# HGRN2 elementwise work on VectorE instead of GpSimd, and a new order of the input projection's columns

## The reference

```python
h = rms_norm(x, norm_pre_mix[l])
proj = jnp.einsum('btd,de->bte', h, w_in[l])        # 3400 columns, the last 2048 are hq, hf, hi, hg
...
f = lb + (1.0 - lb) * jax.nn.sigmoid(hf)
logf = jnp.log(f)
k = 1.0 - f
q = jax.nn.silu(hq)
# S_t = diag(f_t) S_{t-1} + k_t v_t^T,  o_t = S_t^T q_t   (v = hi)
o = rms_norm(o, out_gain) * jax.nn.silu(hg)
```

## Time and profile before

| | us |
|---|---|
| median of 3 runs | 3892.73 (3880.02 to 3896.85) |
| profiled execution, its time | 3889.4 |
| profiled execution, its span | 3887.5 |
| PE busy in the span | 3430.1 (88%) |
| DVE busy | 1858.7 (48%) |
| ACT busy | 1480.8 (38%) |
| POOL busy | 795.1 (20%) |

### The profile page before, as it was taken

One profiled execution on the slowest core, in us unless ns is written; L12 is line 12 of the kernel. 1 busy time (PEld: TensorE's weight loads), 2 busy tenths in 40 slices (PEclk: granted clock), 3 DMA queues, 4 the chain that ended last, 5 costly groups with the idle time before them and its releaser, 6 DMA issues. The chain is left out here.

```text
span 3887.5 us, 45027 instructions
## 1 busy us (share of the span) xinstructions
PE 3430.1 (88%) x17952; PEld 2966.0 (76%) x17952; DVE 1858.7 (48%) x2624; ACT 1480.8 (38%) x2010; POOL 795.1 (20%) x825
## 2 busy tenths in 40 slices
PE   8898998896657788788888897999999999999998
PEld 8898888895646667666667786888788878887887
DVE  3343444443447878888886333332333233323332
ACT  3433434333335555566665433222222222223221
POOL 0456575666731121010000010000000000000000
PEclk9999999998866878989998998999999999999999
DMA  5333232222110000000000344223323332323232
GB/s 181 130 121 110 94 139 96 105 104 74 35 43 20 21 20 11 18 13 11 11 4 4 140 169 155 90 96 135 114 102 116 121 116 98 125 103 119 98 119 87
DMA packets 82982, 336.70 MB, mean 87 GB/s; under 512 B 7264, under 2 KB 28384, under 8 KB 64352
## 3 DMA queue, kind: packets, MB, share of 16 engines
q1 hardware_dynamic: 75872, 312.96, 22.8%
q10 hardware_dynamic: 6912, 20.97, 1.4%
HBM read 272.50 MB, written 61.41 MB: 86 GB/s over the span
## 5 line engine op out<-in xcount | busy, mean ns | idle before, releaser
L1852 PE MATMUL ps_dense<-h_hi,wd_hi 128*128 128x512 f32 x1408 | 551.9, 392 | 31.5 <-DVE h_lo L1802 19.1
L1853 PE MATMUL ps_dense<-h_lo,wd_hi 128*128 128x512 f32 x1408 | 550.9, 391 | 0.0
L1854 PE MATMUL ps_dense<-h_hi,wd_lo 128*128 128x512 f32 x1408 | 550.8, 391 | 0.0
L1796 DVE TENSOR_TENSOR wd_lo<-wd_raw,wd_hi 128x2048 fp32r<-128x2048 f32 (+1 forms) x136 | 303.3, 2230 | 499.8 <-ACT wd_hi L1751 499.8
L667 PE MATMUL PJ<-w_hi,h_hi 128*128 128x342 f32 (+1 forms) x1280 | 423.7, 331 | 4.2 <-DVE w_lo L548 4.2
L668 PE MATMUL PJ<-w_lo,h_hi 128*128 128x342 f32 (+1 forms) x1280 | 415.7, 325 | 0.0
L669 PE MATMUL PJ<-w_hi,h_lo 128*128 128x342 f32 (+1 forms) x1280 | 414.6, 324 | 0.0
L1751 ACT ACTIVATE wd_hi<-wd_raw 128x2048 fp32r<-128x2048 f32 (+1 forms) x136 | 252.5, 1857 | 405.6 <-PE ps_dense L1874 234.7
L1317 PE MATMUL SC<-V,pT 128*128 128x64 f32 x2176 | 332.9, 309 | 42.2 <-ACT pT L1055 42.1
L1317 PEld LDWEIGHTS SC<-V,pT 128*128 128x128 f32 x2176 | 310.7, 222 | 77.7 <-ACT pT L1055 77.7
L1852 PEld LDWEIGHTS ps_dense<-h_hi,wd_hi 128*128 128x128 f32 x1408 | 266.0, 189 | 89.6 <-DVE h_lo L1802 19.5
(11 more groups left out here) (209 smaller groups left out, 6702.5 us busy)
## 6 DMA issues: line engine op xcount, KB each, us to landing
wd_raw<-in_w_gu SPq DMA_DIRECT2D x88, 1024.0 KB, 4.8
wd_raw<-in_w_down SPq DMA_DIRECT2D x40, 1024.0 KB, 4.8
w_raw<-in_w_in SPq DMA_DIRECT2D x20, 1368.0 KB, 6.2
w_raw<-in_w_in SPq DMA_DIRECT2D x20, 1352.0 KB, 6.1
row_h<-proj_d SPq DMA_DIRECT2D x16, 1024.0 KB, 7.9
proj_d<-stage SPq DMA_DIRECT2D x40, 342.0 KB, 3.7
proj_d<-stage SPq DMA_DIRECT2D x40, 338.0 KB, 2.6
row<-proj_d SPq DMA_DIRECT2D x16, 676.0 KB, 4.1
```

The lines of the kernel that those rows point to most:

```text
L1796: nc.vector.tensor_tensor(w_lo[:, k % 2, w], w_raw[:, w], w_hi[:, k % 2, w].bitcast(F32), ALU.subtract).then_inc(w_lo_ready, 1)
L1852: nc.tensor.matmul(o, w_hi[:, f % 2, w], h_hi[:, c, :], start=(c == 0), stop=False)
L1853: nc.tensor.matmul(o, w_hi[:, f % 2, w], h_lo[:, c, :], start=False, stop=False)
L1854: last = nc.tensor.matmul(o, w_lo[:, f % 2, w], h_hi[:, c, :], start=False, stop=(c == KD - 1))
```

## The change

1. All of the recurrence's 512-column and larger elementwise work moves from POOL to DVE: `gates`, `log_low`, `tail_keys`, `output_gate`, `ke`, `level_sum`. POOL keeps the `root` and `norm` steps on a few columns. Two pairs of multiply and add become one SCALAR_TENSOR_TENSOR each (`hq` and `gg`), and the three halvings of `level_sum` become one TENSOR_REDUCE over the eight masks, read with a stride of 128 elements, into a new tile `asum`.
2. On PE `output` is split: `carried` (state part) stands right behind `levels`, and `output` (the part that waits for the sum) stands later. A new semaphore `hs_done` tells DVE that `qe` is free.
3. The projection goes by passes: superblocks 0 and 1 as before, then the HGRN2 columns of superblock 2, those of superblock 3, the attention columns of superblock 3, and last those of superblock 2. `begin` becomes 29, 39, 50, 61, 72, 82, 92, 102, 112, and 6 products for each of blocks 8 to 15. There are five loads of x tiles in place of four (20 tiles, not 16), as superblock 2 is normalised and turned twice.

```diff
-    begin = [29 + 10 * b for b in range(13)] + [149 + 11 * n // 4 for n in range(1, 4)] + [NPROD]
+    PASSES = [(0, HG_COLS), (0, AT_COLS), (1, HG_COLS), (1, AT_COLS), (2, HG_COLS), (3, HG_COLS),
+              (3, AT_COLS), (2, AT_COLS)]
+    chunks = [(s, col) for s, cols in PASSES for col in cols]
...
+    begin = [29 + 43 * b // 4 for b in range(4)] + [72 + 10 * b for b in range(4)] + [112 + 6 * b for b in range(9)]
...
-    row_before = [max(PER * (b // 4) + 24, begin[b - 1] + begin[b - 1] % 2 if b >= 2 else 0) for b in range(NB)]
+    row_before = [max(4 * rows_at[b // 4], begin[b - 1] + begin[b - 1] % 2 if b >= 2 else 0) for b in range(NB)]
...
+            def gates(b):
...
+                link(v.tensor_tensor(fg[:], sig[:, 1, :], lb[:, 1, :], ALU.mult))
+                link(v.tensor_tensor(hk[:], lb[:, 1, :], fg[:], ALU.subtract))
+                v.tensor_tensor(fg[:], lb[:, 0, :], fg[:], ALU.add).then_inc(hk_ready, 1)
+                v.scalar_tensor_tensor(hq[:], sig[:, 0, :], 1.0, r[:, H_ROW["q"]:H_ROW["q"] + 512], ALU.add,
+                                       ALU.mult).then_inc(hq_ready, 1)
...
+                link(v.scalar_tensor_tensor(gg[:], sig[:, 2, :], 1.0, z, ALU.add, ALU.mult))
+                v.tensor_tensor(gg[:], gg[:], g_hg[:], ALU.mult).then_inc(gg_ready, 1)
...
-            def level_queries(b, h):
+            def level_operands(b, h):
                 n = HG * b + h
                 wait_pair_read(dve, use[f"decay{h}", b])
                 v.tensor_copy(elast[:, h:h + 1], decay[:, h % 2, NM - 1, P - 1:P])
                 if n >= 2:
-                    dve.wait_ge(ho_done, n - 1)
+                    dve.wait_ge(hs_done, n - 1)
                 v.tensor_tensor(qe[:, h % 2], decay[:, h % 2], hqT[:, h:h + 1, :].broadcast_to([P, NM, P]),
                                 ALU.mult).then_inc(qe_ready, 1)
+                v.tensor_tensor(ke[:, h % 2], decay[:, h % 2, 0:NM - 1, :],
+                                hkT[:, h:h + 1, :].broadcast_to([P, NM - 1, P]), ALU.mult).then_inc(ke_ready, 1)
...
                 v.tensor_tensor(am[:, h % 2], heads(pair((f"level{h}", b)), NM), pick[:], ALU.mult)\
                  .then_inc(sa_free_dve, 1)
+                wait_pair_read(dve, use[f"level{h}", b])
+                if n >= 2:
+                    dve.wait_ge(ho_done, n - 1)
+                v.tensor_reduce(asum[:, h % 2, :], am[:, h % 2].rearrange("p m t -> p t m"), AX_X, ALU.add)\
+                 .then_inc(am_ready, 1)
```

More of the change, by code:

```diff
@@ L86, in project_hgrn_phase @@
 def project_hgrn_phase(nc, a, proj_d, mix_d):
-    BL = NB // 4
-    PER = 4 * NC_IN
-    NPROD = 4 * PER
+    HG_COLS, AT_COLS = list(range(NH_IN)), list(range(NH_IN, NC_IN))
+    PASSES = [(0, HG_COLS), (0, AT_COLS), (1, HG_COLS), (1, AT_COLS), (2, HG_COLS), (3, HG_COLS),
+              (3, AT_COLS), (2, AT_COLS)]
+    chunks = [(s, col) for s, cols in PASSES for col in cols]
+    NPROD = 4 * len(chunks)
+    rows_at = {}
+    for n, (s, col) in enumerate(chunks):
+        if col == NH_IN - 1:
+            rows_at[s] = n + 1
     SLOTS = 9
-    begin = [29 + 10 * b for b in range(13)] + [149 + 11 * n // 4 for n in range(1, 4)] + [NPROD]
+    begin = [29 + 43 * b // 4 for b in range(4)] + [72 + 10 * b for b in range(4)] + [112 + 6 * b for b in range(9)]
     slot_end = lambda b, k: begin[b] + (k + 1) * (begin[b + 1] - begin[b]) // SLOTS
[L95 to L102, removed]
+    tiles, turned_after, normed_at, loaded_at, uses_tile = list(range(4)), {0: 2, 1: 3}, {}, {}, {}
+    for i in range(4):
+        uses_tile[i] = i
+    for c in range(1, len(chunks)):
+        if chunks[c][0] != chunks[c - 1][0]:
+            for i, (load, norm) in enumerate(((-20, -11), (-18, -9), (-16, -7), (-4, -2))):
+                e = len(tiles)
+                tiles.append(4 * chunks[c][0] + i)
+                turned_after[4 * c - 4 + i] = e
+                normed_at[4 * c + norm] = e
+                loaded_at.setdefault(4 * c + load, []).append(e)
+                uses_tile[4 * c + i] = e
+    NT = len(tiles)
     with ExitStack() as ctx:
@@ L148, in project_hgrn_phase @@
         am = sb("am", [P, 2, NM, P])
+        asum = sb("asum", [P, 2, P])
         elast = sb("elast", [P, HG])
@@ L288, in _ @@
                     load_w(chunk_of(n) + 2)
-                for t in range(4, NB):
-                    if n == PER * (t // 4 - 1) + (10, 12, 14, 36)[t % 4]:
-                        load_x(t)
+                for e in loaded_at.get(n, []):
+                    load_x(e)
                 for b in range(NB):
@@ L316, in dense @@
                         root(normed_at[n])
[L318 to L348, removed]
@@ L710, in levels, with carried @@
                 t.matmul(out[:, NM - 1, :], hkT[:, h, :], hqT[:, h, :], start=True, stop=True).then_inc(sa_full, 1)
-            def output(b, h):
+            def carried(b, h):
                 if h == 0 and b >= 1:
@@ L716, in output @@
                     wait_pair_read(pe, use["kv", b - 1])
-                to = heads(SD[:])[:, h, :]
-                t.matmul(to, qe[:, h % 2, NM - 1, :], state[:, b % 2, h, :], start=True, stop=False)
+                t.matmul(heads(SD[:])[:, h, :], qe[:, h % 2, NM - 1, :], state[:, b % 2, h, :], start=(h == 0), stop=False)\
+                 .then_inc(hs_done, 1)
+            def output(b, h):
                 pe.wait_ge(am_ready, HG * b + h + 1)
                 v = heads(row[:, b % 2, H_ROW["i"]:H_ROW["i"] + 512])
-                t.matmul(to, am[:, h % 2, 0, :], v[:, h, :], start=False, stop=True).then_inc(ho_done, 1)
+                t.matmul(heads(SD[:])[:, h, :], asum[:, h % 2, :], v[:, h, :], start=False, stop=(h == HG - 1)).then_inc(ho_done, 1)
             def key_values(b):
@@ L744, in _ @@
                 levels(b, 0)
+                carried(b, 0)
                 dense(slot_end(b, 2), slot_end(b, 3))
@@ L748, in _ @@
                 levels(b, 1)
-                output(b, 0)
+                carried(b, 1)
                 dense(slot_end(b, 4), slot_end(b, 5))
                 decays(b, 3)
+                output(b, 0)
                 dense(slot_end(b, 5), slot_end(b, 6))
                 levels(b, 2)
+                carried(b, 2)
                 output(b, 1)
@@ L756, in _ @@
                 levels(b, 3)
-                output(b, 2)
+                carried(b, 3)
                 key_values(b)
                 dense(slot_end(b, 7), slot_end(b, 8))
+                output(b, 2)
                 output(b, 3)
```

106 lines of the change are left out of this document (49 added, 57 removed).

## The result

The changed kernel takes 3762.86 us (median of 4 runs, 3761.64 to 3767.61) against 3890.3 us for four runs of the kernel before (3880.02 to 3896.85). The ratio is 0.9677, with a 95% interval of 0.9653 to 0.9701: 127 us less. The forecast was 3770.

A forecast was written before the change was run, and what follows sets the result against it. PE and its waits bound blocks 0 to 11, the recurrence's chain the last four. 947.5 us becomes 455 + 362 = 817; with the head 134 less, 12 back for hops: 3770, forecast 3740 to 3800 (0.68), range 3735 to 3835.

The forecast's parts named there:

- Head: Before block 0, PE's wait for the first `hq`: 6.3 us of POOL operations become 2.8 on DVE, gain 3.5 us.
- Blocks 0 to 7: 513.4 us, less 60 for the sum wait, plus 16 for added PE work, less 15 for clock: 455 us.
- hops: Steps between engines that the walk leaves out, all blocks: 0.75 us a block, 12 us given back.
- Blocks 8 to 15: Six products each: four blocks at 47.1 us and four at 40.5, 350, plus 12 for the second preparation: 362 us.
- Even blocks: Blocks 8, 10, 12, 14: last `output` waits behind `fg_lo`, which waits for ACT; 44.4 us plus 2.7 for clock.
- The preparation: Superblock 2's second preparation, within blocks 8 to 15: four turns on PE and 10 us on DVE, +12 us.
- The 2.7 us for the clock: Even blocks, behind the stall: ten-odd matmuls at the slow pace and the block's last steps, some 2.7 us.
- dear strided sum: Rival: the mask sum on DVE costs about twice the contiguous one, +37 us in blocks 8 to 15, 3807; chance 0.10.
- the slower rival: Slower than before if the sum takes about 5 us, each microsecond costing 32 in blocks 8 to 15; chance 0.04.
- DVE's order: Rival: blocks 8 to 15 each lose 7 to 8 us at `fg_lo` or behind `gates`, about 3830; chance 0.10.
- the change would do nothing: Rival: six-product blocks run no shorter than 64 us, the last eight taking 512, total 3909; chance 0.03.
- The remark on late rows: Gates of blocks 4, 8, 12: rows now come early enough, no cost; a late row would stop DVE's queue.

The follow-up runs named there:

- one_prep: Changed kernel without superblock 2's second preparation; its last four chunks use superblock 3's tiles, so its attention columns come out wrong: 3751.74 us, ratio 0.9648.
- log_first: Changed kernel with ACT making the next block's logarithm right behind its gates, ahead of two slots of copies and weights: 3749.28 us, ratio 0.963.
- turned_sum: Changed kernel with `am` written masks innermost, so the reduction reads contiguous floats and the multiply writes with a step of 8: 3772.87 us, ratio 0.9689.
- double_sum: Changed kernel with every mask sum made twice, the first into a tile that nothing reads: 3802.23 us, ratio 0.9765.
- halved_sum: Changed kernel with the mask sum as three contiguous halvings on DVE in place of the strided reduction: 3762.48 us, ratio 0.9665.

## Why the prediction was right

The mechanism held: the wait on the sum went, DVE had room for the work with small waits, and the order gave the last blocks their products. That 3763 lies within 7 us of 3770 is partly luck, as the terms below show.

**Head.** 3.5 us foretold, 1.5 found. The step was priced rightly: from the start of the gates' first operation to PE's start it is 2.8 us on DVE and was 6.4 on POOL. But the row came later in this profile, which is ACT's first `sig`, after and before:

```profile
135.39 1.06 ACT L391 ACTIVATE sig<-row_h 128x1024 f32<-128x1024 f32 x1 [11.86 <-DMA row_h<-proj_d]
```

```profile
133.77 1.06 ACT L449 ACTIVATE sig<-row_h 128x1024 f32<-128x1024 f32 x1 [9.83 <-DMA row_h<-proj_d]
```

`one_prep`, the same up to there, has its first `hqT` at 141.93, not 143.05, so part of these 1.6 us is scatter.

**Blocks 0 to 7.** 455 us and some 6 for hops foretold, 464.1 found. The wait on the sum went, all of it. The clock came back further than I took (0.98). What I had not seen is the 9.4 us at the key products, where PE waits for a buffer that `h_lo` frees: I had costed DVE's list as fitting into the block, and it fits, but its one wait for ACT, walked for the even blocks of the second half only, delays `h_lo` here. With that wait out of the way (`log_first`) the eight blocks were no shorter, so it did not set their time by itself.

**Blocks 8 to 15.** 362 us and 6 for hops foretold, 353.1 found. Even blocks were to take 47.1 us: blocks 8, 10 and 14 took 46.0, 45.8 and 45.8, with the stall at the place and from the cause named. Odd ones were to take 40.5: without the second preparation, blocks 9, 11 and 13 took 40.8, 40.5 and 41.3. The last took 37.4; I had counted it as an odd one. It ends at `osb`, which in block 10 comes 1.8 us before the next `hqT`, and it has no next block's gates to make. The preparation was 9.7, not 12. The 2.7 us for the clock was too dear. From the waiting matmul to the first product it is 5.6 us in block 10 (736.83 to 742.45), and 4.5 us one block earlier behind a wait of 0.48 us. So it cost 1.1 us, since part of the slow stretch lay where PE would have waited for `hkT`. Against that, block 10's walk was 1.2 us short at the last `output` (45.2, not 43.9): some hops had to be added, but fewer than 0.75 us in each block, as the odd blocks ran only 0.4 us over in the mean.

**Where the working was wrong.** Two steps of it failed. The sum was priced at 1.25 us "as both read one element at a time" and took 1.98. The Trainium skill's rule ("Advanced Engine Details and Errata", Memory Cachelines), weighed and set aside in the prediction, was the better guide: the same instruction takes 1.22 us on contiguous data in `turned_sum`. The rival "dear strided sum" thus came true for most of its price, but not for its time. Its "+37, all on the path in blocks 8 to 15" took a microsecond of DVE as a microsecond of the block. `double_sum` shows a half of it there, and `halved_sum` at most a sixth for time taken away. In an even block three of the four sums lie ahead of `fg_lo`, which waits for ACT in any case. At my slope the measured price would have added 23 us, for a forecast of 3793; at `double_sum`'s it adds 12. The forecast has neither. What hid the missing term in blocks 8 to 15 are terms that were too large: 6 us for hops, 6 for the clock in four even blocks, 3 for the last block and 2 for the preparation. So these blocks came out 15 us below the forecast although a cost was left out. That is luck. The same slope stands in the slower rival ("4 x 8 = 32 us" for each microsecond), so its turning point was put too near; no run went that far.

**The other rivals.** DVE's order cost no 7 to 8 us a block: `fg_lo` waited 11.4 us in all of the last eight. That the change would do nothing, with six-product blocks no shorter than 64 us, is excluded: they take 44.1 in the mean. The remark on late rows, filed under what costs nothing, held for this order and may be a part of its worth: with the old order the late rows do stop DVE's queue at the gates (28 us), as the prediction said that they would.

**The signs.** The last `osb` was to be near 970 and is at 960.20; blocks 0 to 7 were to take 56 to 58 us and take 58.0; `qe` and the clock are as said. TENSOR_REDUCE at 1.2 to 1.3 us is the sign that failed, and its 1.98 lies just under the 2 us that I had set as the mark of being wrong.

## What to carry to other kernels

When an engine's work moves into another's queue, look for the waits in that queue and for what is queued behind each. Here moving one ACT step took 13 us from the phase, a faster sum alone 2.6 at most, and behind the moved step the same faster sum 9.2. Price a microsecond of an engine that is nearly full by doubling the suspected operation once: it was worth 0.5 on the block here, and not 1 or 0. Free a double buffer as soon as its last reader can run, and look twice before a slow access pattern goes on the step that frees one.

## What the runs showed of the hardware

- A reduction over 1024 fp32 elements read with a step of 512 bytes took 1.98 us on VectorE, and 1.22 us on contiguous ones; a multiply of 1024 elements took 1.22 us, and 2.15 us when it wrote with a step of 32 bytes. So the step cost 0.76 us where it was read and 0.93 where it was written, for 1024 elements.
- SCALAR_TENSOR_TENSOR on 512 fp32 elements took 0.68 to 0.69 us, no more than the plain multiply, so a fused pair cost one here.
- Two multiplies with both inputs in SBUF, on VectorE and GpSimd at once, took 3.07 and 2.12 us in the median; on VectorE one after the other they took 1.22 and 1.08. The shortest on GpSimd was 2.08, so it is the one on VectorE that waited.
- Behind a stall of 5.28 us on TensorE the matmuls of the opening ran at the slow pace (four transposes in 1.06 us, 0.60 behind a shorter wait) until 742.45, 5.6 us in all. It cost 1.1 us, as the next wait was shorter for it.
